# One step of a hybrid streaming encoder on eight cores: handover rows on another queue, x read back a head earlier, forget-gate logits in two buffers, transposes one step later, squares on two engines

## What is computed

```python
h = modulate(rmsnorm(x, g_ffn1), sh1, sc1)
x = x + 0.5 * gt1 * swiglu(h, w_ffn1_in, w_ffn1_out)      # d_ff 2816
h = modulate(rmsnorm(x, g_mix), sh2, sc2)
z = h @ w_in               # q, k, v, forget logits f (16), B, C, X, gates GA, GC
logf = log_sigmoid(z_f + b_f);  F = cumsum([past_logf, logf])
p = softmax(causal(q k^T / 8 + F_q - F_k));  o_attn = p v  # with cached k, v
u = C * X;  o_conv = B * short_conv(u, w, 3)
m = sigmoid(GA) * o_attn + sigmoid(GC) * o_conv
x = x + gt2 * (m @ w_out)
h = modulate(rmsnorm(x, g_ffn2), sh3, sc3)
x = x + 0.5 * gt3 * swiglu(h, w_ffn2_in, w_ffn2_out)
y = rmsnorm(x, g_final)    # outputs y, k, v, logf, last two u
```

## Time and profile before

| | us |
|---|---|
| time, median of 3 runs | 1934.12 (1933.35 to 1935.08) |
| the profiled execution: its own time | 1932.67 |
| its span on core 5, the slowest (0 to 7: 1922.3 to 1931.0) | 1931.0 |
| PE busy on core 5 | 1812.7 (94%) |
| ACT, DVE, POOL busy | 768.1, 760.4, 134.5 |

### The profile page before, as it was taken

The page is one execution under the profiler, slowest core; times in us unless marked ns, Lnnn a source line. Parts: engine busy times, 40 slices in busy tenths (PEclk is TensorE's granted clock), DMA queues, the critical chain, the costliest instruction groups (busy, mean ns, idle before and its releaser), DMA issues.

```text
span 1931.0 us, 35563 instructions; the slowest of 8 cores (1922.3 to 1931.0 us)
## 1 busy us (share of the span) xinstructions
PE 1812.7 (94%) x13360; PEld 963.7 (50%) x13360; DVE 760.4 (39%) x1401; ACT 768.1 (40%) x1496; POOL 134.5 (7%) x221
## 2 busy tenths in 40 slices
PE   3799999999996699999999999998999999999997
PEld 1345545554453365656565656554444444544443
DVE  1243233122465345545455454543552223322255
ACT  2563100111464465565555656565661110011132
POOL 2002000110014100000000000000000000000000
PEclk7899999999999799999999999999999999999998
DMA  9604504893224332313132322213522220422012
GB/s 175 190 4 67 96 0 77 138 159 60 98 79 105 71 80 46 80 36 81 35 81 46 92 47 69 61 32 73 168 44 44 38 34 1 76 34 34 17 66 120
DMA packets 42262, 137.91 MB, mean 71 GB/s; under 512 B 5456, under 2 KB 7856, under 8 KB 38992
## 3 DMA queue, kind: packets, MB, share of 16 engines
q0 software_dynamic: 25328, 80.99, 25.5%
q1 hardware_dynamic: 16768, 54.65, 8.0%
HBM read 180.18 MB, written 36.22 MB: 112 GB/s over the span
## 4 chain that ended last, share of the span: by engine, by line
PE 85%; DMA 5%; DVE 4%; ACT 3%; issue 2%; POOL 1%; DVEq 0%; SPq 0%; ACTq 0%; POOLq 0%
PE pb L461 81%; PE pb L459 3%; DMA RG<-w_ada 2%; DVE tw L633 1%; DMA RX<-xs 1%; DMA RX<-xT 1%; DMA fd<-RX 1%; DVE RX L684 1%; ACT tw L471 1%; PE pb L1246 1%; ACT scr L471 1%; DMA kT<-RX 0%; ACT H L471 0%; DVE RX L645 0%; ACT RG L471 0%
## 5 line engine op out<-in xcount | busy, mean ns | idle before, releaser
L461 PE MATMUL pb<-H,wsall 128*128 128x512 bf16 (+1 forms) x5760 | 1154.4, 349 | 19.9 <-ACT RX L471 6.0
L461 PEld LDWEIGHTS pb<-H,wsall 128*128 128x128 bf16 x5760 | 510.1, 98 | 517.5 <-issue 43.2
L471 ACT ACTIVATE tw<-pb 128x512 bf16<-128x512 f32 (+3 forms) x320 | 169.2, 532 | 650.7 <-PE pb L461 641.3
L471 ACT ACTIVATE RG<-pb 128x512 bf16<-128x512 f32 (+3 forms) x688 | 344.5, 531 | 186.3 <-PE pb L461 160.5
L461 PE MATMUL pb<-RG,wsall 128*128 128x512 bf16 (+1 forms) x2080 | 388.3, 348 | 9.4 <-DVE RX L684 9.0
L670 DVE TENSOR_TENSOR RG<-pb,tw 128x512 bf16<-128x512 f32 (+1 forms) x218 | 132.8, 611 | 484.3 <-PE pb L461 423.1
L461 PEld LDWEIGHTS pb<-RG,wsall 128*128 128x128 bf16 x2080 | 186.7, 98 | 208.5 <-issue 13.7
L461 PE MATMUL pb<-RX 68*128 68x512 bf16 (+3 forms) x640 | 215.4, 350 | 26.0 <-ACT RX L471 26.0
L459 PEld LDWEIGHTS pb<-RX,RG 128*128 128x128 bf16 x2176 | 139.4, 97 | 108.0 <-issue 7.3
L684 DVE SCALAR_TENSOR_TENSOR RX<-pb,DER,RX 128x512 f32<-128x512 f32 (+1 forms) x192 | 112.4, 594 | 187.4 <-PE pb L461 182.1
L459 PE MATMUL pb<-RX,RG 128*128 128x65 bf16 x2176 | 169.8, 193 | 2.8 <-ACT RG L471 2.4
(11 more groups left out here) (97 smaller groups left out, 701.7 us busy)
## 6 DMA issues: line engine op xcount, KB each, us to landing
wsall<-w_in POOLq DMA_DIRECT2D x32, 512.0 KB, 6.9
wsall<-w_ada POOLq DMA_DIRECT2D x28, 512.0 KB, 12.2
wsall<-w1i POOLq DMA_DIRECT2D x22, 512.0 KB, 17.7
wsall<-w2i POOLq DMA_DIRECT2D x22, 512.0 KB, 9.4
RX<-xT SPq DMA_DIRECT2D x4, 2048.0 KB
xs<-RX SPq DMA_DIRECT2D x4, 2048.0 KB
kT<-RX SPq DMA_DIRECT2D x32, 256.0 KB
vo<-RX SPq DMA_DIRECT2D x32, 256.0 KB
```

The costliest lines, as they stand in the source:

```text
L461: ins = e.matmul(o, lhsT=l, rhs=r, start=st, stop=sp)
L471: return P.op("scalar", lambda e: e.activation(out=out, in_=in_, func=func, **kw), reads=reads, writes=writes)
```

## The change

It has five parts.
1. Front: the squares of block 1 with odd k are made by VectorE; its statistics stand behind j = 4 instead of 3, its `n_mod` one place later (the last three behind j = 6). `PRE` has one more entry for that.
2. Handover: FT1, FT2 and FH get a second buffer in RG; `sums` runs four ticks after the products; the memsets and `cache_loads(0)` stand before the first v unit; `row_loads(0)` is called at the end of the last `sums` and issued by POOL.
3. The cached rows (fcd) of the two streams have a buffer record each (`B_kcrow[s]`).
4. `transpose_out` runs three ticks after `finish`, not two.
5. x of blocks 0 and 1 is loaded back when head 7 begins.

```diff
@@ line 338 of before @@
         fx = lambda off, n: RX[0:16, (2 * CH + off) // 4:(2 * CH + off) // 4 + n]
-        FT1, FT2, FR = fx(0, 512), fx(2048, 512), fx(6144, 512)
+        FR = fx(6144, 512)
+        FT1S = [fx(0, 512), RG[0:16, 1536:2560].bitcast(F32)]
+        FT2S = [fx(2048, 512), RG[0:16, 2560:3584].bitcast(F32)]
         FLFS = [fx(4096, 512), RX[0:16, 13312 // 4:13312 // 4 + 512]]
         FFB = [fx(8192, 512), fx(10240, 512)]
-        FH = RX[0:16, (2 * CH + 12288) // 4:(2 * CH + 12288) // 4 + 768].bitcast(BF16).rearrange(
-            "p (r t) -> p r t", r=3)
+        FHS = [RX[0:16, (2 * CH + 12288) // 4:(2 * CH + 12288) // 4 + 768].bitcast(BF16).rearrange(
+            "p (r t) -> p r t", r=3), RG[0:16, 0:1536].rearrange("p (r t) -> p r t", r=3)]
         mv = RG[:, 0:8 * NT].rearrange("p (k t) -> p k t", k=8)
@@ line 613 of before @@
 
-        def n_sq(tb, k):
+        def n_sq(tb, k, on_vec=False):
             n = TBS[tb][1]
+            if on_vec:
+                vec(lambda e: e.tensor_tensor(out=SQB[k][:, 0:n], in0=xt(k, tb), in1=xt(k, tb), op=ALU.mult),
+                    [XB[k][tb]], [B_sq[k]])
+                return
             act(SQB[k][:, 0:n], xt(k, tb), AF.Square, [XB[k][tb]], [B_sq[k]])
@@ line 792 of before @@
         many = lambda what, lo, hi: [(what, k) for k in range(lo, hi)]
-        PRE = [[[], [], many("sq", 0, 4), many("sq", 4, 8), many("mod", 0, 2), many("mod", 2, 5), many("mod", 5, 8)],
-               [many("sq", 0, 4), many("sq", 4, 8), [], many("mod", 0, 3), many("mod", 3, 6), many("mod", 6, 8), []]]
+        PRE = [[[], [], many("sq", 0, 4), many("sq", 4, 8), [], many("mod", 0, 2), many("mod", 2, 5), many("mod", 5, 8)],
+               [many("sq", 0, 4), many("sq", 4, 8), [], many("mod", 0, 3), many("mod", 3, 6), many("mod", 6, 8), [], []]]
         sums = [cached_sum(0, 0), cached_sum(0, 1), None, None]
+        def ahead(tb, j):
+            for what, k in PRE[tb > 0][j]:
+                if what == "sq":
+                    n_sq(tb + 1, k, tb == 0 and k % 2 == 1)
+                else:
+                    n_mod(tb + 1, k, 0, 0)
+
         for tb in range(5):
@@ line 798 of before @@
                 if tb < 4:
-                    for what, k in PRE[tb > 0][j]:
-                        if what == "sq":
-                            n_sq(tb + 1, k)
-                        else:
-                            n_mod(tb + 1, k, 0, 0)
+                    ahead(tb, j)
                 if tb > 0 or j > 1:
                     ffn_in("w1i", j, tb)
-                if tb < 4 and j == (3, 1)[tb > 0]:
+                if tb < 4 and j == (4, 1)[tb > 0]:
                     n_stats(tb + 1)
+                if tb < 4 and j == JB1 - 1:
+                    ahead(tb, JB1)
                 if tb > 0 and j == 0:
...
@@ line 872 of before @@
         seed_set0()
-        alias_seed(flat(MB) + B_pt + [B_u, B_upad], allg)
-        alias_seed([B_kc, B_kcrow, B_kcone], [WSB[0], WSB[1]])
+        alias_seed(flat(MB) + B_pt + [B_u, B_upad, B_fhs[1], B_ft1s[1], B_ft2s[1]], allg)
+        alias_seed([B_kc, B_kcone] + B_kcrow, [WSB[0], WSB[1]])
         ring.owner[0] = ring.owner[1] = "kc"
@@ line 890 of before @@
             FLF, B_flf = FLFS[tb % 2], B_flfs[tb % 2]
+            FH, B_fh = FHS[tb % 2], B_fhs[tb % 2]
+            FT1, B_ft1 = FT1S[tb % 2], B_ft1s[tb % 2]
+            FT2, B_ft2 = FT2S[tb % 2], B_ft2s[tb % 2]
             bank = nxt_of("p", P_BANKS)
@@ line 905 of before @@
             def sums():
+                if tb == 4:
+                    last_sums()
+                    row_loads(0)
+                    return
+                last_sums()
+
+            def last_sums():
                 vec(lambda e: e.scalar_tensor_tensor(out=FLF[:, 0:n], in0=FT1[:, 0:n], scalar=0.0, in1=FT2[:, 0:n],
@@ line 925 of before @@
             later(1, logits)
-            later(3, sums)
+            later(4, sums)
 
@@ line 936 of before @@
             st = c % 2
-            P.dma("sync", lambda e: e.dma_start(out=q_aug[st][64:65, :, :], in_=fd[0:1, 2 * c:2 * c + 2, :]),
+            q_ = "gpsimd" if c == 0 else "sync"
+            P.dma(q_, lambda e: e.dma_start(out=q_aug[st][64:65, :, :], in_=fd[0:1, 2 * c:2 * c + 2, :]),
                   reads=B_fd + [B_qone[st]], writes=[B_qrow[st]])
-            P.dma("sync", lambda e: e.dma_start(out=k_aug[st][65:68, :, :], in_=fd[:, 2 * c:2 * c + 2, :]),
+            P.dma(q_, lambda e: e.dma_start(out=k_aug[st][65:68, :, :], in_=fd[:, 2 * c:2 * c + 2, :]),
                   reads=B_fd + [B_kone[st]], writes=[B_krow[st]])
@@ line 950 of before @@
                     out=kc_aug[65:68, s, :, :], in_=fcd[:, 2 * c:2 * c + 2, s, :]),
-                    reads=B_fcd + [B_kcone], writes=[B_kcrow])
+                    reads=B_fcd + [B_kcone], writes=[B_kcrow[s]])
             later(12, lambda: vec(lambda e: e.tensor_copy(out=vc_ext[:, :, :, :, 0:64], in_=VST), [B_vst], [B_vc]))
@@ line 1236 of before @@
             if hh == 1:
-                later(2, lambda: transpose_out(c, qb, x_, 4))
+                later(3, lambda: transpose_out(c, qb, x_, 4))
 
@@ line 1291 of before @@
                                   qa[0:68, hh, qc:qc + SQ], True, True) for i in range(4) for hh in range(2)]
-                        mm(items, [B_kc, B_kcrow, B_kcone] + [B_q[st_][hh][4] for hh in range(2)] +
+                        mm(items, [B_kc, B_kcrow[s], B_kcone] + [B_q[st_][hh][4] for hh in range(2)] +
                            [B_qrow[st_], B_qone[st_]], [PBB[b]])
@@ line 1373 of before @@
 
+        pool_set = lambda fn, writes: P.op("gpsimd", fn, writes=writes)
+        pool_set(lambda e: e.memset(kc_aug[64:68, :, :, :].bitcast(F32), bfpair(-1.0)), [B_kcone] + B_kcrow)
+        pool_set(lambda e: e.memset(U[:, 0:2], 0.0), [B_u])
         run_mods(wrap(k_units(0, 0)), 0)
@@ line 1377 of before @@
         modq.extend([lambda k=k: n_mod(3, k, 1, 3) for k in range(8)])
+        alias_seed([B_vst, B_vc, B_vcone], B_sq)
+        pool_set(lambda e: e.memset(vc_ext[:, :, :, :, 64:66].bitcast(F32), bfpair(2.0)), [B_vcone])
+        cache_loads(0)
         run_mods(wrap(v_units(0, 0)), 2)
@@ line 1390 of before @@
             run_mods(wrap(q_units(0, tb, True)))
-        row_loads(0)
-        alias_seed([B_vst, B_vc, B_vcone], B_sq)
-        pool_set = lambda fn, writes: P.op("gpsimd", fn, writes=writes)
-        pool_set(lambda e: e.memset(kc_aug[64:68, :, :, :].bitcast(F32), bfpair(-1.0)), [B_kcone, B_kcrow])
-        pool_set(lambda e: e.memset(vc_ext[:, :, :, :, 64:66].bitcast(F32), bfpair(2.0)), [B_vcone])
-        pool_set(lambda e: e.memset(U[:, 0:2], 0.0), [B_u])
-        cache_loads(0)
         run_mods(wrap(k_units(0, 3)) + wrap(v_units(0, 3)) + wrap(k_units(0, 4)) + wrap(v_units(0, 4, last=True)))
@@ line 1401 of before @@
         alias_seed(flat(B_q[1]) + [B_qrow[1], B_qone[1]] + B_v[1] + [B_vone[1]],
-                   xcol(2) + [B_ft1, B_ft2, B_flfs[0], B_fr, B_fh] + B_ff)
+                   xcol(2) + [B_ft1s[0], B_ft2s[0], B_flfs[0], B_fr, B_fhs[0]] + B_ff)
+        alias_seed(B_ob, B_fhs[0:1] + B_ff + [B_fr])
+        alias_seed(MB[0] + MB[1], [B_fhs[1], B_ft1s[1], B_ft2s[1]])
         const_rows(1)
@@ line 1408 of before @@
 
+        def reload_x(tb, srcs):
+            n = TBS[tb][1]
+            alias_seed(xcol(tb), srcs)
+            sl_ = slice(XOFF[tb], XOFF[tb] + 8 * n)
+            P.dma("sync", lambda e: e.dma_start(out=RX[:, sl_], in_=xs[:, sl_]), writes=xcol(tb),
+                  waits=[spill[tb]])
+        def reload_early():
+            reload_x(0, flat(B_q[0]) + [B_qrow[0], B_qone[0], B_flfs[1]] + B_v[0] + [B_vone[0]])
+            reload_x(1, flat(B_k[0]) + [B_krow[0], B_kone[0]] + B_stg)
+
         LA = 2
@@ line 1450 of before @@
                     ncur = c
+                    if c == 7:
+                        reload_early()
                     side_q.extend(side_list[c])
@@ line 1487 of before @@
 
-        def reload_x(tb, srcs):
-            n = TBS[tb][1]
-            alias_seed(xcol(tb), srcs)
-            sl_ = slice(XOFF[tb], XOFF[tb] + 8 * n)
-            P.dma("sync", lambda e: e.dma_start(out=RX[:, sl_], in_=xs[:, sl_]), writes=xcol(tb),
-                  waits=[spill[tb]])
-        reload_x(0, flat(B_q[0]) + [B_qrow[0], B_qone[0]] + B_v[0] + [B_vone[0]])
-        reload_x(1, flat(B_k[0]) + [B_krow[0], B_kone[0]] + B_stg)
         reload_x(2, flat(B_q[1]) + [B_qrow[1], B_qone[1]] + B_v[1] + [B_vone[1]] + B_ob)
@@ line 1498 of before @@
         reload_x(4, B_ta)
-        alias_seed([WSB[0], WSB[1]], [B_kc, B_kcrow, B_kcone])
+        alias_seed([WSB[0], WSB[1]], [B_kc, B_kcone] + B_kcrow)
         ring.done("kc")
```

More of the change, by code:

```diff
@@ L851, in build_program @@
         B_ta = [Buf() for _ in range(5)]
-        B_ft1, B_ft2, B_fr, B_fh = [Buf() for _ in range(4)]
+        B_ft1s, B_ft2s, B_fr = [Buf(), Buf()], [Buf(), Buf()], Buf()
+        B_fhs = [Buf(), Buf()]
         B_flfs = [Buf(), Buf()]
@@ L857, in build_program @@
```

(8 more changed lines are left out.)

## The result

The changed kernel took 1898.12, 1899.38 and 1901.08 us, the kernel before 1933.33 to 1935.08 us; the ratio is 0.9822, with a 95% interval of 0.9803 to 0.9841. (Runs in which the cores of one die were granted a lower clock and took longer are left out, here and in all that follows.) The prediction was 1898, with a range of 1888 to 1908. The profiled execution took 1898.12 us.

What follows compares the result with a forecast made beforehand. TensorE, busy 94% of core 5's span, was taken as the bound. Core 5: 20 + 9.5 + 6.8 + 1.2 = 37.5 us, giving 1893.5; core 0: 32.2, giving 1896.1; plus 3.1 is 1899, 1898 taken, range 1888 to 1908.

Steps and rivals of the forecast that it cites:

- Handover: From projections to attention: first score product at 624 instead of 644.06 on core 5; gain 17 to 24 us, 20 taken.
- the third needs FH[0], hence the first write landed ... near 605.5: POOL's third split in the handover waits for the first fd write, which lands near 605.5 behind two 512 KB loads.
- they go too: TensorE's small handover waits, 8.5 us from VectorE standing in sums for a logarithm just issued, vanish with sums a step later.
- no kT wait on ScalarE: Sign of being right: in the handover ScalarE no longer waits for a kT store; its 23.68 us wait goes.
- Transposes: In attention, transposes a step later remove TensorE's waits for them in 15 places: 6.8 us, lower bound 3.
- x back early: End of attention: the 7.24 us wait for x goes, plus clock loss after it: 9.5 us on core 5, 7.3 on core 0.
- Squares and statistics: Front, block 1: squares on two engines and later statistics gain 1.2 us on core 5, lose 1.9 on core 0.
- Cache rows: Cache-row loads booked singly: up to 3.8 us less on SP in each head, worth nothing in total time.
- No line: Rival: the first fd write slips past POOL's loads; handover at 620.4, 4 us more gained, time 1894; chance 0.15.
- the handover passes to another wait: Rival: VectorE's vc copy or slow row loads (9.5 us) put the first product at 632; time 1906; chance 0.15.
- the transposes did what they are meant to: Denies the rival that the later transposes only move the wait to the gate's bank: 0 of 6.8, 1905; chance 0.06.
- no side unit lost a bank: Denies the rival "slower": later transposes keep side units from their bank in 34 places, 1939 at 1.0 us each; chance 0.02.

Runs made afterwards that it cites:

- h_late: Changed kernel with head 0's cache loads (kcT, vc) issued behind the handover's last row load, not ahead of the splits: 1895.45 to 1898.33 us, ratio 0.9803 to the kernel before.
- u_lg3: Changed kernel with the sums three steps behind the forget product again, not four: 1899.28 to 1901.49 us, ratio 0.9815 to the kernel before.
- u_tr2: Changed kernel with the transposes two steps behind again, not three: 1906.39 to 1909.06 us, ratio 0.9859 to the kernel before.
- u_x: Changed kernel with the first two reloads of x issued behind the last attention step again: 1908.3 to 1909.64 us, ratio 0.9865 to the kernel before.
- u_kc: Changed kernel with a head's two cache-row loads booked on one buffer again: 1900.59 to 1902.4 us, ratio 0.9821 to the kernel before.
- h_lf3: Changed kernel with head 0's cache loads behind its row loads, block 3's split on VectorE and, newly, a third lf buffer: 1893.68 to 1896.18 us, ratio 0.9791.

## Why the prediction was right

**Handover.** Forecast: first score product at 624 on core 5, 20 us earlier; measured 624.28, 19.8 earlier. Of these, 2.2 came from the front (1.1 of them because x landed earlier), while the forecast had started from an unmoved front; from A to S it was 17.6 us on core 5 and 15.4 in the mean, where 20 had been forecast. So the instant agrees by luck in part. Two steps under the number were wrong. First, "the third needs FH[0], hence the first write landed ... near 605.5": on core 5 the third cast began at 604.89, but behind VectorE, which waited for the lf store, a small store on SP's queue that the prediction didn't look at. The write had landed at 603.7 (594.69 + 9.0), 1.2 us before the cast. On cores 3, 4 and 6 it did come last, by under 0.5 us. The cause that it named, kcT and vc ahead in POOL's queue, is only the half: they also slow what stands in SP's queue. h_late shows both, 9.0 to 4.3 us for fd and 14.80 to 9.33 for lf. The Trainium skill (DMA: Bandwidth & Descriptors, section Queues, rings and completion order) says that a DMA engine takes turns between the queues it has work for, packet by packet; a store on SP would then not stand behind the whole line of POOL's loads, but be slowed while it lasts, together with the kT and vo stores ahead of it on SP. That fits lf, which landed at 602.5 while vc landed at 603.3 (580.65 + 22.6), but so would a single line for both queues; no run here tells the two apart. The busy share of the DMA engines of the changed kernel, core 5, 574 to 604 us, in tenths over 40 slices, shows both queues' work filling them until then:

```profile
DMA  9899999993969999998798979989998999999984
```

Second, "they go too", of the small waits: VectorE's waits for a logarithm (2.56, 2.34, 2.34 and 1.65 us at L906 before) did go, but waits for kT, vo and lf stores took their place, so TensorE's stayed at 8.7 us; they cost nothing (u_lg3). By the same rows the sign "no kT wait on ScalarE" failed: the wait of 23.68 us went, but three were left, 5.1 us in all. The pace of a split (5.9 us from the third cast to the issue of its write, 5.0 to the next, 5.5 taken), the last write's issue (618.64, forecast 619.4) and the rows' landing (623.9, forecast 624.3) came as worked out.

**Transposes.** 6.8 us forecast; S to T fell by 8.8, of which 8.3 return in u_tr2. Right in mechanism, undersized mainly by the cost of a stop beyond its recorded wait.

**x back early.** 9.5 on core 5 and 7.3 on core 0 forecast, 8.4 and 8.8 measured. The wait went (u_x). The sum also booked a whole return of the clock after it; part of that loss is still there, now behind the 1.33 us wait of the last transposes: 72 matmuls after it took 17.39 us on core 5 and 15.70 on core 1. The granted clock tells the two apart: between 1312 and 1316 us it was 0.66, 0.50, 0.50 and 0.64 in successive microseconds on core 5, the lower level, and it was 1.00 from 1314.0 to 1329.8 on core 1. For these 70 to 72 matmuls five cores took 17.0 to 17.4 us, three 15.5 to 15.7.

```profile
1314.08 15.70 PE L463 MATMUL pb<-RG,wsall 128*128 128x512 bf16 x72
```

```profile
1312.21 17.39 PE L463 MATMUL pb<-RG,wsall 128*128 128x512 bf16 x72
```

**Squares and statistics.** Forecast +1.2 on core 5 and -1.9 on core 0. From the landing of x to A core 5 went from 24.25 to 23.22 us (+1.0), core 0 from 22.56 to 23.21 (-0.65); in the mean nothing. (The rows end the statistics at 68.5 and 67.0, not 68.4 and 66.9; that changes nothing.) **Cache rows**: nothing, as forecast (u_kc).

**Rivals.** "No line" (620.4) is refuted by the first write's 9.0 us, 4.3 in h_late; "the handover passes to another wait" didn't come: the rows landed 2.52 us after the second load's issue, not 9.5, and VectorE's copy of vc at 605.47 held nothing; the transposes did what they are meant to; TensorE's only recorded waits between 660 and 1340 us on core 5 are 2.2 us in 13 places for exponentials and those named above, so no side unit lost a bank. That core 0 would be the slowest was wrong: core 3 was, by 2 us, and core 0's x landed 1.7 us earlier than before.

The mechanisms were right in the main, but that the number came so close is luck. The errors offset one another: +2.4 us at the handover, -1.8 in the transposes, +1.1 at x, -1.0 in front (the earlier x), on core 5 (36.8 us measured, 37.5 forecast). Run again, the same kernel took 1902.1 us in the median (after2), 4 us above the forecast.

## What to carry to other kernels

A small store or load that a chain waits for is as late as the bulk transfers around it, on whatever queue they are: put bulk loads that nobody needs yet behind the chain, as h_late did for some 4.7 us. When a chain of split, store and reload decides, count the buffers of each of its tiles, since one buffer turns every landing into a step (10.5 us here), and read the chain after each fix, because the next single buffer takes over (h_lf3). Value many short waits of TensorE by more than their recorded length (here 0.16 to 0.18 us more each), but only where TensorE is the bound: the same kind of waits in the handover were worth nothing.

## What was unexpected of the hardware

A 32 KB store took 14.80 us to land while the DMA engines were busy to 70% or more in every slice, and 9.33 us with 1 MB of loads fewer ahead. A stop of TensorE cost 0.16 to 0.18 us beyond its recorded wait (15 places, 2.4 to 2.65 us). After a wait of 1.3 us, 72 matmuls took 15.70 us on one core and 17.39 on another, in the same execution, because the granted clock fell to the lower level for some 3 us on the one and not on the other; what decides whether it falls stayed open.
